# The product with w_out as seven block products in two sweeps

## The reference, cut to what matters

```python
    merged = (jax.nn.sigmoid(gate_att) * (y_att @ w_branch_att)
              + jax.nn.sigmoid(gate_dn) * (y_dn @ w_branch_dn))
    return merged @ w_out
...
        y = hybrid_mixer(h, w_in[l], conv_w[l], a_log[l], dt_bias[l], dn_norm[l],
                         w_branch_att[l], w_branch_dn[l], w_out[l])
        x = x + rms_norm(y, post_norm_mix[l])
        h = rms_norm(x, pre_norm_mlp[l])
        y = jnp.square(jax.nn.relu(h @ w_mlp_in[l])) @ w_mlp_out[l]
        x = x + rms_norm(y, post_norm_mlp[l])
```

## Time and profile before

| | |
|---|---|
| time, median of 3 runs | 754.07 us (754.02 to 754.08) |
| time of the profiled execution | 753.69 us |
| its span | 751.9 us |
| TensorE busy | 744.5 us, 99% |
| VectorE busy | 418.1 us, 56% |
| ScalarE busy | 383.9 us, 51% |
| GpSimd busy | 322.6 us, 43% |
| mean granted TensorE clock | 0.998 of 2.4 GHz |
| bytes moved | 123.45 MB, mean 164 GB/s |

### The profile page before, as it was taken

How to read it: one execution, slowest core, us unless ns; L and a number is a source line. 1 busy time by engine, 2 the same in 40 slices (tenths; PEclk the granted TensorE clock), 3 DMA queues, 4 the chain that set the end, 5 groups by cost and what they waited for, 6 DMA issues and landing times.

```text
span 751.9 us, 12181 instructions
## 1 busy us (share of the span) xinstructions
PE 744.5 (99%) x4180; PEld 610.3 (81%) x4180; DVE 418.1 (56%) x627; ACT 383.9 (51%) x623; POOL 322.6 (43%) x294
## 2 busy tenths in 40 slices
PE   9999999999999999999999999999999999999996
PEld 7788778888877878788887988888888888888885
...
GB/s 329 112 88 208 56 65 117 156 183 173 165 196 156 188 176 210 100 224 211 287 160 42 71 126 141 130 183 168 129 214 129 202 237 189 194 191 159 208 183 113
DMA packets 83214, 123.45 MB, mean 164 GB/s; under 512 B 5824, under 2 KB 44896, under 8 KB 83168
## 3 DMA queue, kind: packets, MB, share of 16 engines
...
## 4 chain that ended last, share of the span: by engine, by line
PE 93%; POOL 3%; ACT 2%; DVE 1%; issue 0%; ACTq 0%; POOLq 0%; DVEq 0%
PE bank L676 28%; PE bank L678 27%; PE bank L677 27%; POOL rsq L1955 2%; PE bank L901 1%; PE bank L924 1%; PE bank L911 1%; POOL w_lo L1961 1%; PE bank L865 1%; PE bank L829 1%; PE bank L697 1%; PE bank L706 1%; PE bank L876 1%; PE bank L933 1%; PE bank L973 0%; PE bank L703 0%
## 5 line engine op out<-in xcount | busy, mean ns | idle before, releaser
L1961 POOL TENSOR_TENSOR w_lo<-raw,w_hi 128x512 fp32r<-128x512 f32 x177 | 229.5, 1305 | 251.5 <-ACT w_hi L1113 249.7
L1113 ACT ACTIVATE w_hi<-raw 128x512 fp32r<-128x512 f32 (+2 forms) x214 | 144.9, 684 | 171.7 <-PE bank L678 160.1
L676 PE MATMUL bank<-h_hi,w_hi 128*128 128x512 f32 (+1 forms) x528 | 208.5, 395 | 0.1
L677 PE MATMUL bank<-h_lo,w_hi 128*128 128x512 f32 (+1 forms) x528 | 204.2, 387 | 0.0
L678 PE MATMUL bank<-h_hi,w_lo 128*128 128x512 f32 (+1 forms) x528 | 204.1, 386 | 0.0
L676 PEld LDWEIGHTS bank<-h_hi,w_hi 128*128 128x128 f32 x528 | 99.2, 188 | 25.0 <-issue 4.0
L678 PEld LDWEIGHTS bank<-h_hi,w_lo 128*128 128x128 f32 x528 | 99.2, 188 | 20.6
L677 PEld LDWEIGHTS bank<-h_lo,w_hi 128*128 128x128 f32 x528 | 99.3, 188 | 18.7
L1492 DVE SCALAR_TENSOR_TENSOR relu_sb<-bank,rs_row 128x512 f32<-128x512 f32 x32 | 20.6, 686 | 126.5 <-PE bank L678 114.8
L2092 POOL TENSOR_SCALAR ssh<-ssy 128x1 f32<-128x1 f32 x4 | 1.0, 238 | 151.6 <-ACT junk L1463 151.6
L676 PE MATMUL bank<-w_hi,h_hi 128*128 128x512 f32 x128 | 50.3, 393 | 0.1
...
## 6 DMA issues: line engine op xcount, KB each, us to landing
...
t_sum<-in_w_mlp_out POOLq DMA_DIRECT2D x12, 1024.0 KB, 10.7
...
```

Source lines behind the costliest of these rows:

```text
L676: pe.matmul(o, s_hi, m_hi, start=start, stop=False, skip_group_check=True)
L677: pe.matmul(o, s_hi, m_lo, start=False, stop=False, skip_group_check=True)
L1113: return a.activation(o, i_, ACT.Copy, scale=scale)
L1961: g.tensor_tensor(w_lo[:, slot, :], raw[:, slot, :], w_hi[:, slot, :].bitcast(F32), ALU.subtract).then_inc(lo_ready, 1)
```

## The change

The product with `w_out` is written with the two halves of the tokens, of each pair of feature blocks, and of the columns as 2 x 2 blocks, in seven block products.

- DVE makes, per channel pair g, the four blocks and four sums of them (`m_mix`, eight tiles of 128 x 256). ACT and DVE split them into `o1_hi`/`o1_lo` (four of them, for sweep one) and `o2_hi`/`o2_lo` (three, for sweep two).
- Four weight sums are made in DRAM (`o_copy`, `o_add`, 1 MB each), at the places 48, 52, 60 and 87 among the units, where chunks of the MLP's sums stood.
- Sweep one (`out_one`) takes four products for each of four g; a unit now is 6 matmuls. Then ACT and DVE combine the banks (`x_o`, `y_o`, seeds), and sweep two (`out_two`) takes three products on 12 weight blocks that have tiles of their own (`wo_hi`, `wo_lo`); POOL makes the low parts of the first four, DVE of the others.
- Six of the MLP's chunks keep places before the MLP (`SUM_AT`), the other ten are in its input (`SUM_IN`), whose loops on SP and POOL are written out.
- SP loads the norm vectors behind unit `U_DN + 3`, `x_res` behind `U_DN + 5`, the blocks of sweep two behind `U_DN + 7` and on, and `raw_x` behind all of them.
- The banks are squared in the order 1, 3, 4, 6, 0, 2, 5, 7.

```diff
-SUM_AT = {48 + 13 * i + (0, 4, 12)[q]: (q, i) for i in range(N_SUM) for q in range(3)}
+OUT_SUM_AT = {48: 0, 52: 1, 60: 2, 87: 3}
+SUM_AT = {61: (0, 0), 65: (1, 0), 73: (2, 0), 74: (0, 1), 78: (1, 1), 86: (2, 1)}
+SUM_IN = {3: (0, 2), 4: (0, 3), 5: (1, 2), 6: (1, 3), 7: (2, 2), 8: (2, 3), 11: (3, 0), 12: (3, 1), 13: (3, 2), 14: (3, 3)}
+OUT_ONE = [("p1", "q5", "p7", "q6")] * 3 + [("p1", "q6", "p7", "q5")]
+OUT_BANK = {"p1": (4, 6), "q5": (5, 7), "p7": (0, 2), "q6": (1, 3)}
+OUT_TWO = (((4, 6), 1), ((0, 2), 0), ((5, 7), 2))
...
+        def out_one(g, j):
+            u, s, c = U_BR + 4 * g + j, j, OUT_ONE[g][j]
+            pe.wait_ge(lo_ready, u + 1)
+            if j == 0:
+                pe.wait_ge(o1lo_ready, g + 1)
+            if g == 0:
...
+                elif c in ("p7", "q6"):
+                    pe.wait_ge(prod_ready, 15 if c == "p7" else 16)
+            for i2 in range(2):
+                w = slice(i2 * P, i2 * P + P)
+                x_ = three(bank[OUT_BANK[c][i2]][:], o1_hi[:, g, OUT_A[c], w], o1_lo[:, g, OUT_A[c], w],
+                           w_hi[:, s, :], w_lo[:, s, :], g == 0, g == 3)
+            x_.then_inc(unit_done, 1)
...
+            if u - U_DN in (4, 6, 9, 14):
+                mix_one((4, 6, 9, 14).index(u - U_DN))
+            if u - U_DN in (7, 10, 11, 15):
+                mix_two((7, 10, 11, 15).index(u - U_DN))
+            if u - U_DN in (4, 5, 6, 7, 12, 13, 16):
+                split_out((4, 5, 6, 7, 12, 13, 16).index(u - U_DN))
...
         for g in range(4):
             v.wait_ge(gates_ready, 8 + 2 * g + 2)
             v.wait_ge(unit_done, U_DN + 2 * g + 2)
             for m in range(2):
                 mark(v.tensor_tensor(m_d[:, m, :], bank[g % 2 * 2 + m][:], gate_d[:, 2 * g + m, :], ALU.mult), prod_ready)
+            if g == 3:
+                o1_low(1)
             for m in range(2):
-                mark(v.tensor_tensor(m_a[:, m, :], m_d[:, m, :], gate_a[:, 2 * g + m, :], ALU.add), m_ready)
...
+                i_ = v.tensor_tensor(m_mix[g][:, 5 * m:5 * m + 2, :].rearrange("p a c -> p (a c)"), m_d[:, m, :],
+                                     gate_a[:, 2 * g + m, :], ALU.add)
...
+            s1 = v.tensor_tensor(x[4], x[0], x[5], ALU.subtract)
+            v.tensor_tensor(x[3], x[1], x[0], ALU.subtract)
+            link(s1)
+            mark(v.tensor_tensor(x[2], x[1], x[4], ALU.subtract), mix1_ready)
+            v.tensor_tensor(x[7], x[6], x[2], ALU.subtract).then_inc(mix2_ready, 1)
+            if g == 1:
+                o1_low(0)
+        o1_low(2)
+        o1_low(3)
+        for g in range(4):
+            o2_low(g)
+        for e in range(4, 7):
+            wo_low(e)
...
         for u in range(U_DN, U_OUT - LEAD):
             split_u(u + LEAD)
+            if 4 <= u - U_DN < 8:
+                e = u - U_DN - 4
+                g.wait_ge(wohi_ready, e + 1)
+                g.tensor_tensor(wo_lo[e][:], wo_raw[e][:], wo_hi[e][:].bitcast(F32), ALU.subtract).then_inc(wolo_first, 1)
```

More of the change, by code:

```diff
@@ L246, in program @@
     y_lo = at("y_lo", 144, [P, 4, S], F32R)
-    m_a = at("m_a", 160, [P, 2, S])
-    m_d = at("m_d", 164, [P, 2, S])
+    o1_hi = at("o1_hi", 0, [P, 4, 4, 256], F32R)
+    o1_lo = at("o1_lo", 16, [P, 4, 4, 256], F32R)
+    o2_hi = at("o2_hi", 56, [P, 4, 4, 256], F32R)
+    o2_lo = at("o2_lo", 112, [P, 4, 4, 256], F32R)
+    m_d = at("m_d", 72, [P, 2, S])
+    m_mix = [at(f"m_mix{g}", kb, [P, 8, 256]) for g, kb in enumerate((136, 152, 160, 168))]
+    x_o = at("x_o", 160, [P, 2, 512])
+    y_o = at("y_o", 164, [P, 2, 512])
+    wo_at = (184, 188, 192, 76, 128, 132, 144, 148, 136, 140, 152, 156)
+    wo_hi = [at(f"wo_hi{e}", kb, [P, 512], F32R) for e, kb in enumerate(wo_at)]
+    wo_raw = [at(f"wo_raw{e}", kb + 2, [P, 512]) for e, kb in enumerate(wo_at)]
+    wo_lo = [at(f"wo_lo{e}", kb + 2, [P, 512], F32R) for e, kb in enumerate(wo_at)]
     x_res = at("x_res", 96, [P, NT, D])
@@ L754, in unit, with out_two @@
                                   k == 0, k == 3)
[L755 to L758 removed]
             i.then_inc(unit_done, 1)
[L761 to L766 removed]
+        def out_one(g, j):
[4 more added lines that the diff above has]
+            if g == 0:
+                if c == "p1":
+                    for f in (FILLS - 4, FILLS - 3, FILLS - 2, FILLS - 1):
+                        freed(pe, f)
+                elif c in ("p7", "q6"):
[5 more added lines that the diff above has]
+            x_.then_inc(unit_done, 1)
+        def out_two(p, i2, gs=range(4)):
+            banks, a_ = OUT_TWO[p]
+            w = slice(i2 * P, i2 * P + P)
+            for g in gs:
+                e = 4 * p + g
+                if i2 == 0:
+                    if p == 0:
+                        pe.wait_ge(wolo_first, g + 1)
+                        pe.wait_ge(o2lo_ready, g + 1)
+                    else:
+                        pe.wait_ge(wolo_ready, e - 3)
+                x_ = three(bank[banks[i2]][:], o2_hi[:, g, a_, w], o2_lo[:, g, a_, w], wo_hi[e][:], wo_lo[e][:],
+                           False, g == 3)
+            return x_
         def side_step(name, i):
@@ L1735, in _, with mix, o1_low, o2_low @@
                 side_step(name, i)
+        def mix(g):
+            return [m_mix[g][:, s, :] for s in range(8)]
+        def o1_low(g):
+            v.wait_ge(o1hi_ready, g + 1)
+            v.tensor_tensor(o1_lo[:, g, :, :], m_mix[g][:, 1:5, :], o1_hi[:, g, :, :].bitcast(F32),
+                            ALU.subtract).then_inc(o1lo_ready, 1)
+        def o2_low(g):
+            v.wait_ge(o2hi_ready, g + 1)
+            v.tensor_tensor(o2_lo[:, g, 0:3, :], m_mix[g][:, 5:8, :], o2_hi[:, g, 0:3, :].bitcast(F32),
+                            ALU.subtract).then_inc(o2lo_ready, 1)
+        def wo_low(e):
+            v.wait_ge(wohi_ready, e + 1)
+            v.tensor_tensor(wo_lo[e][:], wo_raw[e][:], wo_hi[e][:].bitcast(F32), ALU.subtract).then_inc(wolo_ready, 1)
         for g in range(4):
@@ new lines, in _ @@
+        for i2 in range(2):
+            v.wait_ge(p1_copied, i2 + 1)
+            v.wait_ge(unit_done, U_OUT - 2)
+            mark(v.tensor_tensor(x_o[:, i2, :], bank[1 + 2 * i2][:], x_o[:, i2, :], ALU.subtract), x_made)
+        for i2 in range(2):
+            v.wait_ge(unit_done, U_OUT - 1)
+            v.tensor_tensor(y_o[:, i2, :], x_o[:, i2, :], bank[2 * i2][:], ALU.subtract).then_inc(y_made, 1)
+        v.wait_ge(y_made, 2)
+        for i2 in range(2):
+            v.wait_ge(unit_done, U_OUT)
+            v.tensor_tensor(bank[1 + 2 * i2][:], y_o[:, i2, :], bank[5 + 2 * i2][:], ALU.add).then_inc(c22_made, 1)
@@ L1749, in _, with scaled @@
+        for i2 in range(2):
+            v.tensor_tensor(bank[5 + 2 * i2][:], x_o[:, i2, :], bank[5 + 2 * i2][:], ALU.add).then_inc(z_seeded, 1)
+        for e in range(7, 12):
+            wo_low(e)
         v.wait_ge(xr_in, 16)
         v.wait_ge(pn_in, 32)
-        def scaled(t, pn, s0):
-            for half in range(2):
+        def scaled(t, pn, halves=range(2)):
+            for half in halves:
                 b = 2 * t + half
                 c = slice(half * 512, half * 512 + 512)
-                v.wait_ge(ssy_ready, s0 + b + 1)
+                v.wait_ge(ssy_ready, SQUARED.index(b) + 1)
@@ L1875, in _ @@
         two(1)
-        v.wait_ge(y_made, 2)
+        v.wait_ge(y_made, 4)
         for i2 in range(2):
```

251 lines of the change are left out of this document (147 added, 104 removed).

## The result

| | before | changed |
|---|---|---|
| time, median of 4 runs each | 754.05 us (753.89 to 754.08) | 763.23 us (761.97 to 763.70) |
| profiled execution, its span | 753.69 us, 751.9 us | 763.25 us, 761.5 us |
| TensorE busy | 744.5 us, 99% | 744.2 us, 98% |
| VectorE, GpSimd busy | 418.1 us, 322.6 us | 460.0 us, 341.9 us |
| mean granted clock | 0.998 | 0.992 |

The changed kernel is slower: ratio 1.0123, 95% interval 1.0110 to 1.0135. The forecast was 763.0 us, in a range of 752 to 768. The page shows TensorE with 24 matmuls fewer and hardly less busy time, mostly since a matmul at half clock counts double.

A forecast was written before the change was run, and what follows sets the result against it. The prediction took TensorE, busy 99%, to bound the kernel. Its terms, -5.44 + 12.3 + 2.5 + 0.4 less 0.4, gave +9.3 us (9.1 by layout) on 753.69; forecast 763.0 us, range 752 to 768.

The forecast's parts named there:

- What is taken out: Sweeps one and two: 168 matmuls instead of 192, 5.44 us less on TensorE's path.
- The first wait: Third product of sweep one: TensorE waits some 6.4 us for the 15th product m_d, delayed by eight VectorE-GpSimd collisions.
- The rest of sweep one: Sweep one ends at 404.0 instead of 391.7: 12.3 us of waits, 6.4 at the third product, 3 for o1_low(2).
- (c): Rival: the first wait drops TensorE's clock to half, up to 5 us more, 768; chance of more 0.06.
- The floor: Sweep one: work through the shared port puts the last w_lo at 398.5 at the earliest, 8 us later than without waits.
- Sweep two: VectorE reaches x_o and y_o about 12 us late; 2.5 us wait at the transposes, 0.4 more at the first MLP matmul.
- The sum: Whole kernel: -5.44 + 12.3 + 2.5 + 0.4, less 0.4 of earlier small waits: +9.3 us, forecast 763.0.
- Moves costed at nothing: Moved MLP chunks, w_out's sums and SP's load order cost nothing; w_hi of U_DN+6 some 2 us later, still in time.
- the exclusion: Shared SBUF port: VectorE operations with two SBUF inputs and GpSimd's w_lo take turns; a collision costs 1.06 us.
- The signs: Trace marks: waits for m_d over 4 us, o1_lo 2 or more, sums over 1.5, w_lo above 1.29, MLP near 425.
- (a): Rival: four collisions or fewer before the third product, so the gain stays, 749 us; chance 0.12.
- (b): Rival: waits at g=0 and g=2 total only 4 to 8 us through better overlap, 753 to 757; chance 0.12.

The follow-up runs named there:

- e1: Changed kernel without GpSimd's four wo_lo of sweep two's first blocks, their matmuls taking the high part twice: 759.65 us.
- e2: Changed kernel with the products m_d written back into their PSUM bank and the eight sums reading that bank: 761.33 us.
- e4: Changed kernel with TensorE kept busy by 24 extra matmuls in the first long wait and 9 before the transposes: 761.98 us.
- e5: Kernel before with only the moves: MLP chunks, w_out's sums made but unused, norm vectors and x_res at the changed kernel's places: 756.02 us.
- e7: Changed kernel with x_res loaded in four pieces of 512 KB instead of one of 2 MB: 761.83 us.
- c1: Changed kernel with sums and two of four differences of pairs 0 to 2 reading PSUM, x_res in pieces, some wo_lo moved: 753.73 us.
- c3: c1 with VectorE's operations in another order, wo_lo redistributed between VectorE and GpSimd, no ACT operation moved ahead of a w_hi it could delay: 751.90 us.

## Why the prediction was right, and where it was not

**What is taken out.** Right: 168 instead of 192 matmuls.

**The first wait.** The step "eight collisions at 1.06 us, 8.5 us: m_d ends at about 379" held: from 360.5 on the rows of VectorE show nine, which cost 9.4 us over the durations alone (0.42 for a difference, 0.69 for a sum, 1.22 for `o1_lo`), and the 15th product ended at 379.1. One collision more and a chain that was 0.9 us shorter without them (9.1 us from 360.5, not 9.7 from 360.8) cancel. The wait was 5.91 instead of 6.4 us. TensorE stood idle 6.1 us beyond its pace between 373.13 and 379.20. e1 and e2 show that the mechanism is the one named.

**The rest of sweep one.** Sweep one was put at 404.0 and ended at 403.50: 33.6 us for 96 matmuls of 21.8, a loss of 11.8 us against 12.3. Inside it the parts were otherwise. The 3 us for `o1_low(2)` did not appear as a wait, because ten matmuls at half clock lost 10 x 0.2 = 2.0 us in front of it; e4 shows it as 2.48 us once those ten run at full clock. Rival (c) had foreseen this ("the next wait gives back up to 3 us of what they lose"), and put its own price on top at up to 5 us; at this place it was nothing. 0.4 us were lost at the start (370.32), which the sum did not have. The floor is borne out: it put the last `w_lo` at 398.5 with about 4 us of idle port on top, and GpSimd ended it at 401.96.

**Sweep two.** 66 matmuls from 403.50 end at 418.5, the transposes began at 421.07: 2.6 us against 2.5. From the transposes to the MLP it took 4.86 us, before 3.42: 1.44 us against the 0.4 of the sum. This term was mis-sized, by the clock's second fall, which the prediction looked for only behind the wait of 6.4 us.

**The sum.** -5.44 + 11.8 + 2.6 + 1.44, less 0.7 us that stood there before (186 matmuls from 369.92 would have put the transposes at 412.1, they came at 412.80): +9.7 us, as measured. The forecast had +9.3, and +9.1 by its layout. In the medians the difference is 9.2 us. That the forecast of 763.0 lies 0.2 us from the median is partly luck: 0.5 us too much in sweep one and 1.0 too little behind the transposes work against each other, and the changed kernel's own runs go from 761.97 to 763.70.

**Moves costed at nothing.** This step failed in its reason and held in its result. (It counts three sums of `w_out`; there are four, all at places where chunks stood.) It asked whether TensorE would miss the late `w_hi` ("still about 1 us ahead of its need") and not who stood behind it on ACT. By itself the move costs 2.5 us (e5). In the changed kernel taking it back moved neither the first wait nor the transposes to an earlier time (e7), since GpSimd then met VectorE earlier. Whether it would cost again once the exclusion is relieved no run shows; c1 took both.

**The signs.** Right: the wait for `m_d`, `w_lo` above 1.29 us, the MLP near 425. Wrong: the sums' mean is 1.1 and not over 1.5 us, three differences of four have a mean under 1 us (956, 915 and 688 ns), GpSimd has idle time, and no wait for `o1_lo` in the third group. Collisions come in runs: where GpSimd is idle for lack of `w_hi` (377.4 to 379.7, 381.0 to 382.9), VectorE's operations take 0.42 us, or 1.28 for two sums, again, and a mean over all pairs hides it.

**The rivals.** (a) put its border at four collisions; by its own slack of 2.1 us it would be two. The trace has nine, so either way it falls. c3 shows how much of it was had: 1.9 us of the 5.4. (b) had its condition met and its price missed: the waits at g=0 and g=2 come to 5.9 us in all, within its 4 to 8, but the time is not 753 to 757. Between its waits and the time lie what it left out: the half clock behind the first wait (2.0 us), the steps for `w_lo` (about 3 us), and 4.0 us in sweep two and the transposes. (c) came at two places and cost 1.44 us, at the second.
